# Rotary embedding in a two-branch attention block: how the rotated channels change places

## What is computed

```
def partial_rope(t, pos):
    half = ROT_DIM // 2
    inv_freq = jnp.power(jnp.float32(ROPE_THETA),
                         -jnp.arange(0, ROT_DIM, 2, dtype=jnp.float32) / ROT_DIM)
    ang = pos.astype(jnp.float32)[:, None] * inv_freq[None, :]
    cos = jnp.cos(ang)[None, :, None, :]
    sin = jnp.sin(ang)[None, :, None, :]
    tf = t.astype(jnp.float32)
    x1, x2, rest = tf[..., :half], tf[..., half:ROT_DIM], tf[..., ROT_DIM:]
    out = jnp.concatenate([x1 * cos - x2 * sin, x2 * cos + x1 * sin, rest], axis=-1)
    return out.astype(t.dtype)
...
        h = rms_norm(x, norm_g[layer])
        proj = jnp.einsum('bsd,de->bse', h, w_in[layer])
        (qa, ka, va, za, qb, kb, vb, zb, ga, gb) = jnp.split(proj, split_pts, axis=-1)
        qa = partial_rope(qa.reshape(b, s, A_Q_HEADS, HEAD_DIM), pos)
        ka = partial_rope(ka.reshape(b, s, A_KV_HEADS, HEAD_DIM), pos)
        va = va.reshape(b, s, A_KV_HEADS, HEAD_DIM)
        ya = swa_sink_attention(qa, ka, va, a_sinks[layer]) * jax.nn.silu(za)
```

## Time and profile before

| what | value |
|---|---|
| median of 3 runs | 3460.74 us (3460.51 to 3461.7) |
| the profiled execution, its time | 3458.64 us |
| its span, first to last instruction | 3456.8 us |
| mean granted TensorE clock | 0.999 |
| busy: PE, PEld, DVE, ACT, POOL | 97%, 72%, 43%, 41%, 38% |
| matmuls | 16456 |
| DMA traffic | 319.63 MB, mean 92 GB/s |

### The profile page before, as it was taken

How to read it: one execution, slowest core, us unless ns; L and a number is a source line. 1 busy time by engine, 2 the same in 40 slices (tenths; PEclk the granted TensorE clock), 3 DMA queues, 4 the chain that set the end, 5 groups by cost and what they waited for, 6 DMA issues and landing times.

```text
span 3456.8 us, 48457 instructions
## 1 busy us (share of the span) xinstructions
PE 3369.6 (97%) x16456; PEld 2502.4 (72%) x16456; DVE 1483.7 (43%) x3113; ACT 1432.5 (41%) x2985; POOL 1313.8 (38%) x1087
## 2 busy tenths in 40 slices
PE   7999999999999999999999999999999999999998
PEld 5667866678666786667866678666786667866686
DVE  5561355513554135541355413554135541355412
ACT  4443344433444334443344434444344443444432
POOL 3334432344323443234532344323443234532244
PEclk9999999999999999999999999999999999999999
DMA  4122421224212242122421124212242112421123
GB/s 145 59 68 87 169 92 50 67 87 165 92 50 67 86 166 92 50 67 86 170 87 54 63 86 171 88 54 62 89 168 92 50 62 92 167 90 49 56 91 116
DMA packets 97788, 319.63 MB, mean 92 GB/s; under 512 B 9984, under 2 KB 26624, under 8 KB 95360
## 3 DMA queue, kind: packets, MB, share of 16 engines
q1 hardware_dynamic: 97536, 316.34, 28.1%
HBM read 299.52 MB, written 16.78 MB: 91 GB/s over the span
## 4 chain that ended last, share of the span: by engine, by line
PE 49%; issue 28%; POOL 13%; DVE 7%; ACT 2%; POOLq 0%; DMA 0%; DVEq 0%; ACTq 0%; SPq 0%
POOL w_lo L746 12%; PE acc L876 10%; PE acc L878 8%; PE acc L877 8%; PE ps_o L969 5%; PE ps_pt L937 4%; PE sc L917 2%; PE sc L908 2%; PE sc L876 1%; PE sc L878 1%; PE sc L877 1%; DVE sc L1212 1%; DVE negm L1220 1%; PE acc L978 1%; DVE probs_t L1286 1%
## 5 line engine op out<-in xcount | busy, mean ns | idle before, releaser
L746 POOL TENSOR_TENSOR w_lo<-w_raw,w_hi 128x512 fp32r<-128x512 f32 x928 | 1211.7, 1311 | 2096.0 <-ACT w_hi L1023 2095.9
L876 PE MATMUL acc<-h_hi,w_hi 128*128 128x512 f32 x2688 | 1117.0, 416 | 16.7 <-DVE q L1273 12.4
L878 PE MATMUL acc<-h_hi,w_lo 128*128 128x512 f32 x2688 | 1054.3, 392 | 0.0
L877 PE MATMUL acc<-h_lo,w_hi 128*128 128x512 f32 x2688 | 1050.8, 391 | 0.0
L1023 ACT ACTIVATE w_hi<-w_raw 128x512 fp32r<-128x512 f32 x928 | 573.5, 624 | 333.8 <-DMA w_raw<-w 104.5
L876 PEld LDWEIGHTS acc<-h_hi,w_hi 128*128 128x128 f32 x2688 | 505.0, 188 | 233.7 <-issue 144.0
L878 PEld LDWEIGHTS acc<-h_hi,w_lo 128*128 128x128 f32 x2688 | 504.9, 188 | 112.6
L877 PEld LDWEIGHTS acc<-h_lo,w_hi 128*128 128x128 f32 x2688 | 506.9, 189 | 83.7
L1105 ACT ACTIVATE probs_b<-sc,negm 128x640 f32<-128x640 f32 x256 | 203.6, 795 | 381.3 <-DVE negm L1220 379.6
L1245 DVE SCALAR_TENSOR_TENSOR part<-th,sc 128x512 f32<-128x512 f32 x64 | 43.9, 686 | 566.5 <-PE sc L878 566.5
L1112 ACT ACTIVATE probs_t<-ps_pt 128x512 f32<-128x512 f32 (+1 forms) x272 | 150.6, 554 | 235.2 <-PE ps_pt L937 235.2
(11 more groups left out here) (119 smaller groups left out, 3566.0 us busy)
## 6 DMA issues: line engine op xcount, KB each, us to landing
w_raw<-w SPq DMA_DIRECT2D x464, 512.0 KB, 3.5
rows<-x SPq DMA_DIRECT2D x36, 512.0 KB, 7.7
xt<-x_t SPq DMA_DIRECT2D x16, 1024.0 KB, 9.9
out<-rows SPq DMA_DIRECT2D x32, 512.0 KB, 2.7
x_in<-x SPq DMA_DIRECT2D x28, 512.0 KB, 5.7
cs<-rope_tab SPq DMA_DIRECT2D x8, 512.0 KB, 4.3
bias<-near SPq DMA_DIRECT2D x1, 1024.0 KB, 13.3
g_out<-final_g SPq DMA_DIRECT2D x1, 512.0 KB, 11.3
```

The source lines that it names most:

```text
L746: pool.tensor_tensor(w_lo[n % 2][:, c], w_raw[n % 2][:, c], w_hi[n % 2][:, c].bitcast(FP32), ALU.subtract).then_inc(w_split, 1)
L876: pe.matmul(dst[:, :], hi, src_hi[:, k, :], start=begin, stop=False)
L877: pe.matmul(dst[:, :], hi, src_lo[:, k, :], start=False, stop=False)
L878: mm = pe.matmul(dst[:, :], lo, src_hi[:, k, :], start=False, stop=end)
```

## The change

The matrix, its two products, the rounding to `pre_hi` and the subtraction `pre_lo` are taken out. A new tile `rot` (128 x 512, zero from the start, in place of the two matrix tiles) receives the rotated channels of `pre` by four DMAs of 8 partitions within SBUF, which swap channels 0 to 7 with 8 to 15 of both heads. SP issues them once ScalarE has evicted the tile; they stand in SP's order where the tile's job stands in the plan. The cosine product is written straight to the destination, the sine product is made in place in `rot` with a table whose sign differs for the two halves, and the sum is taken in the destination. The numbers of lines in the file after are its own.

```
+            def swap(b, step):
+
+
+                wait_freed(sp, b, step)
+                for h0 in (0, HD):
+                    for to, src in ((h0, h0 + HALF_ROT), (h0 + HALF_ROT, h0)):
+                        sp.dma_start(rot[to:to + HALF_ROT, :], pre[src:src + HALF_ROT, :]).then_inc(rope_swapped, 16)
...
+            sp.wait_ge(zeroed, 6)
...
+                    elif step[0] == "job" and step[1] in ("k", "q") and step[2] < PAIRS:
+                        swap(b, step)
...
+            pool.memset(rot[:, :], 0.0).then_inc(zeroed, 1)
...
-                    elif kind in ("rope", "rope_k"):
-                        claim(b, step)
-                        pe.wait_ge(rope_lo, b * NROPE + (ROPE_NO[step] + 1))
-                        pe.matmul(bank(step)[:, :], perm_r[:, :], pre_hi[:, :], start=True, stop=False)
-                        pe.matmul(bank(step)[:, :], perm_r[:, :], pre_lo[:, :], start=False,
-                                  stop=True).then_inc(acc_full, 1)
...
-                    wait_freed(act, b, step)
-                    act.activation(pre_hi[:, :], pre[:, :], ACT.Copy).then_inc(rope_hi, 1)
...
                     elif kind in ("rope_in", "rope_in_k"):
-                        no = ROPE_NO[(kind.replace("_in", ""), step[1])]
-                        dve.wait_ge(rope_hi, b * NROPE + (no + 1))
-                        dve.tensor_tensor(pre_lo[:, :], pre[:, :], pre_hi[:, :].bitcast(FP32),
-                                          ALU.subtract).then_inc(rope_lo, 1)
+                        of_k = kind == "rope_in_k"
+                        wait_freed(dve, b, ("job", "k" if of_k else "q", step[1]))
                         dve.wait_ge(cs_in, 16 * (b + 1))
-                        dve.wait_ge(rope_lo, b * NROPE + (no + 1))
-                        dve.tensor_tensor(pre[:, :], pre[:, :], cs[:, 0, :], ALU.mult).then_inc(rope_cos, 1)
+                        if of_k and not first:
+                            wait_kept(dve, b, "keep_k", PAIRS - 1)
+                        dve.tensor_tensor(roped(step), pre[:, :], cs[:, 0, :], ALU.mult).then_inc(rope_cos, 1)
                     elif kind in ("rope", "rope_k"):
-                        s = step[1]
                         no = ROPE_NO[step]
-                        wait_full(dve, b, step)
-                        if kind == "rope_k" and not first:
-                            wait_kept(dve, b, "keep_k", PAIRS - 1)
-                        dst = k_a[:, P:P + BLK] if kind == "rope_k" else q[POS[s] % 2][:, :]
-                        dve.tensor_tensor(dst, bank(step)[:, :], cs[:, 1, :], ALU.mult).then_inc(free(step), 1)
-                        wait_freed(dve, b, step)
+                        dve.wait_ge(rope_swapped, b * (64 * NROPE) + 64 * (no + 1))
+                        dve.tensor_tensor(rot[:, :], rot[:, :], cs[:, 1, :], ALU.mult).then_inc(rope_sin, 1)
                         dve.wait_ge(rope_cos, b * NROPE + (no + 1))
-                        dve.tensor_tensor(dst, pre[:, :], dst, ALU.add).then_inc(rope_done, 1)
+                        dve.wait_ge(rope_sin, b * NROPE + (no + 1))
+                        dve.tensor_tensor(roped(step), roped(step), rot[:, :], ALU.add).then_inc(rope_done, 1)
```

More of the change, by code:

```diff
@@ L31 @@
 HD = 64
+HALF_ROT = HD // 8
 PAIRS = 4
@@ L266, in check_plan @@
     assert [step[1] for step in PLAN if step[:1] == ("mm",) and step[2] == 0] == list(range(NW))
-USES_ACC = ("job", "turn_v", "rope_k", "rope", "norm")
+USES_ACC = ("job", "turn_v", "norm")
 check_plan()
@@ L357, with program @@
 check_ring()
-def program(nc, x, x_t, w, near, far, sinks, norm_g, final_g, gate_b, rope_tab, perm, eye, out):
+def program(nc, x, x_t, w, near, far, sinks, norm_g, final_g, gate_b, rope_tab, eye, out):
     off = [(nc.sbuf_base + 63) // 64 * 64]
@@ L406, in program @@
     pre = at("pre", [P, BLK], FP32, y_lo_at + 4 * BLK * 3)
-    pre_lo = at("pre_lo", [P, BLK], FP32R, y_lo_at + 4 * BLK * 6)
-    pre_hi = at("pre_hi", [P, BLK], FP32R, y_lo_at + 4 * BLK * 7)
     bias = sb("bias", [P, 9, A_KEYS])
@@ L422, in program @@
     ident = sb("ident", [P, P])
-    perm_raw = sb("perm_raw", [P, P])
-    perm_r = sb("perm_r", [P, P], FP32R)
+    rot = sb("rot", [P, BLK])
     far_sb = sb("far_sb", [P, 8])
@@ L480, in program @@
     pair_valued = sem("pair_valued")
-    rope_hi = sem("rope_hi")
-    rope_lo = sem("rope_lo")
+    rope_swapped = sem("rope_swapped")
     rope_cos = sem("rope_cos")
+    rope_sin = sem("rope_sin")
     rope_done = sem("rope_done")
@@ L512, in program @@
     c_dve = sem("c_dve")
-    N_CONSTS = 6
+    N_CONSTS = 5
     ADDED = HALVES * TT - O_BANKED
@@ L676, in _ @@
             load_w(0, 1)
-            for dst, src in ((perm_raw[:, :], perm), (g_out[:, :], final_g), (bias[:, 0:8, :], near), (far_sb[:, :], far),
+            for dst, src in ((g_out[:, :], final_g), (bias[:, 0:8, :], near), (far_sb[:, :], far),
                              (sink_sb[:, :], sinks), (gb_raw[:, :], gate_b)):
@@ L722, in _ @@
             pool.memset(v_b[:, 0:TT, :], 0.0).then_inc(zeroed, 1)
-            pool.wait_ge(zeroed, 5)
+            pool.memset(rot[:, :], 0.0).then_inc(zeroed, 1)
+            pool.wait_ge(zeroed, 6)
             def rsqrt(which, t, n, got, got_count, mid, done, count):
@@ L817, in _ @@
             turn_rstd(0)
-            pe.wait_ge(zeroed, 5)
+            pe.wait_ge(zeroed, 6)
             def token_products(b, n, c):
@@ L1178, in _ @@
             dve.wait_ge(consts_in, 16 * N_CONSTS)
-            dve.tensor_copy(perm_r[:, :], perm_raw[:, :]).then_inc(c_dve, 1)
             dve.tensor_scalar(gb_half[:, :], gb_raw[:, :], 0.5, None, ALU.mult).then_inc(c_dve, 1)
@@ L1184, in _, with roped @@
             dve.memset(bias[:, 8, :], 0.0).then_inc(c_dve, 1)
-            dve.wait_ge(c_dve, 11)
+            dve.wait_ge(c_dve, 10)
             dve.memset(bias[0:CHUNK, :, A_KEYS - CHUNK:A_KEYS], NEG).then_inc(c_dve, 1)
             dve.memset(bias[CHUNK:P, 8, CHUNK:P], NEG).then_inc(c_dve, 1)
-            dve.wait_ge(c_dve, 13)
+            dve.wait_ge(c_dve, 12)
+            def roped(step):
+                return k_a[:, P:P + BLK] if step[0].endswith("_k") else q[POS[step[1]] % 2][:, :]
             def shape_scores(b, first, s, t, hh):
@@ L1361, in rope_tables @@
     tab[0] = 1.0
-    perm = np.zeros((P, P), np.float32)
     for h0 in (0, HD):
         for i in range(half):
-            for c in (h0 + i, h0 + half + i):
+            for c, sign in ((h0 + i, -1.0), (h0 + half + i, 1.0)):
                 tab[0, c] = np.cos(ang[:, i])
-                tab[1, c] = np.sin(ang[:, i])
-            perm[h0 + half + i, h0 + i] = -1.0
-            perm[h0 + i, h0 + half + i] = 1.0
+                tab[1, c] = sign * np.sin(ang[:, i])
     tab = tab.reshape(2, P, NBLK, BLK).transpose(2, 1, 0, 3)
-    return np.ascontiguousarray(tab), perm
+    return np.ascontiguousarray(tab)
 def kernel(x, norm_g, w_in, a_sinks, b_rel_bias, w_br_a, w_br_b, gate_bias, w_out, final_g):
@@ L1411 @@
     far = np.ascontiguousarray(np.broadcast_to(b_rel_bias[0][:, 2 * P], (P, 8)))
-    rope_tab, perm = rope_tables()
+    rope_tab = rope_tables()
     arrays = {
@@ L1419 @@
         "gate_b": np.ascontiguousarray(gate_bias[0].reshape(2 * KT, P).T),
-        "rope_tab": rope_tab, "perm": perm, "eye": np.eye(P, dtype=np.float32),
+        "rope_tab": rope_tab, "eye": np.eye(P, dtype=np.float32),
     }
```

## The result

| what | before | after |
|---|---|---|
| median of the runs, us | 3461.07 (4 runs, 3460.51 to 3461.7) | 3486.41 (4 runs, 3483.12 to 3488.37) |
| the profiled execution, its time, its span, us | 3458.64, 3456.8 | 3488.37, 3486.6 |
| mean granted TensorE clock | 0.999 | 0.989 |

The ratio of after to before is 1.0074, with a 95% interval of 1.0061 to 1.0087: the change costs 25 us where I had forecast a gain of 26, and the time lies 30 us above the upper end of my range.

A forecast was written before the change was run, and what follows sets the result against it. TensorE was taken to bound the kernel; 22 us from q1 to q3, 0 from the lead and 4 from block 0 gave 26 off 3458.64, so 3432.6, stated as 3435 with 2.1 for the median; range 3400 to 3456.

The forecast's parts named there:

- q1 to q3: 24 rotations inside the attention steps: each gains 0.93 us as ScalarE's tanh and copy come earlier, 22 us in all.
- The pitch: SP's queue: issues some 0.53 us apart, so four take 2.1 and the weight load is asked for at 932.45.
- The landing: Weight load behind the four DMAs: needs 3.3 to 4.1 us, median 3.5, so it lands at 935.95.
- The following one waits for `w_lo` in any case: SP's queue in q1 to q3: only one load is held up; the next waits for GpSimd's `w_lo` anyway.
- slower: Rival, chance 0.09: SP issues at 1.34 us pitch delay weight loads; 24 rotations lose 2.3 us each, about 3525 us.
- three signs: Would make it wrong: `rot` wait over a microsecond, issue pitch over 0.76, or q0's scores starting over 2 us off.
- lead: q0 and k0, blocks 1 to 7: VectorE's chain sets the scores' start; gain 0, 1.5 us either way, 7 times.
- block 0: First block's lead: TensorE's 2.91 us wait for `pre_lo` and the products go, with 0.46 for q0: 4 us gained.
- one long wait in place of two short ones: Lead, blocks 1 to 7: TensorE waits once, behind the sum of q0, 2 to 4 us a block.
- The turn came 0.6 us earlier: q1 to q3: the copy of turned weights ends at 933.13 instead of 933.73, so TensorE is 0.6 us earlier.
- Landing of the small DMAs: Swapping DMAs into `rot`: taken as 3.3 us from weight loads, landing at 935.3; nothing late under 3.8 us.
- VectorE's waits for `rot` near none: Sign expected in the profile after: VectorE hardly waits for the swapped channels.

The follow-up runs named there:

- experiment 2: Kernel before, permutation kept, plus four idle copies of 8 partitions within SBUF where the change has its swaps, behind the same wait: 3479.62 us, ratio 1.0057.
- Experiment 4: Changed kernel plus six unread products ahead of the turn that waits behind z1, z2 and z3, 33 us more work: 3468.72 us, ratio 1.003 to before.
- experiment 1: Changed kernel with each group of four swapping DMAs issued after the next weight load, not ahead of it: 3431.13 us, ratio 0.9919 to before.
- experiment 5: Changed kernel, swap behind the next weight load, and the last row product of the block before moved later in the plan: 3412.52 us, ratio 0.9856 to before.
- experiment 6: Changed kernel, swap behind the next weight load, and k0's sine product and sum moved to the second quarter of q0: 3431.28 us, ratio 0.9917 to before.
- experiment 7: Changed kernel, swap behind the next weight load, with both the last row product and k0's sine product and sum moved later: 3413.02 us, ratio 0.9862 to before.
- experiment 8: Kernel before, permutation kept, with only the last row product of the block before moved later in the plan: 3455.84 us, ratio 0.9985.

## Why the prediction was wrong

The step that failed is the term of **q1 to q3**: "the load is asked for at 932.45", and behind it that it lands 3.5 us later, at 935.95, and that TensorE then waits "some 0.7". Measured from `pre`'s start, that is an issue at 2.75 and a landing at 6.25; after showed an issue at 3.31 to 3.44, a landing at 6.9 to 7.2 in 17 rotations and at 8.1 to 9.0 in 7, and TensorE waiting 1.0 to 1.4 us in 14 of the 17, 3.0 in block 0's three, and 2.2 to 3.1 in the 7. Three things were wrong or missing, in the order of the chain.

1. *The pitch.* I took 0.53 us for an issue, from weight loads. An issue of `rot` takes 0.62 us and the next starts 0.67 to 0.72 after it, in all 24 rotations. The row of SP's queue, after:

```profile
L670 SPq DMA_DIRECT2D rot<-pre x160: 624/625/797, 27.2 to 3231.4; - x160
```

That made each load 0.66 us later than I said, and the tanh 0.7 later (7.52 from `pre`'s start, where I had 6.8). This term alone ate most of the 0.93 us that I counted for each: in blocks 1 to 7 the rotation of q1, which met no packet of 16 KB, gained 0.16 us each (q1 to q2, 416.6 us in place of 417.7).

2. *The landing.* I took "3.3 to 4.1, median 3.5" from the earlier trace rows. That line is of the 20 loads between 900 and 1100 us only; the same line for all 464 of before is

```profile
DMA to landing us min/median/max: 3.3/3.5/10.8
```

and the loads that met a packet, 4.07 to 4.64 us in q2 of before, were there to be seen. *"The following one waits for `w_lo` in any case"* held for its own time: it started 3.9 us after `pre`'s start in blocks 1 to 6, before 4.0. What it left out is that the first load, asked for 8 us ahead of it before, now goes some 0.5 us ahead (3.41 and 3.90 in q2), so two loads share the DMA engines in every rotation. In 17 of 24 that did not matter (3.44 to 3.93 us, where I had 3.5). In the other 7 an instruction packet was there too, and the load took 4.7 to 5.6, more than with a packet alone. I had no term for a load that takes longer, and six of the seven make most of the loss of q2. Why a packet meets these loads in after and none in experiment 2 is open.

3. *The clock.* The prediction has no sentence on it. Behind waits of TensorE of 2.5 to 3.1 us it went to half, 15 times. Experiment 4 shows 18 us of that by itself. Of the 15, seven stand in leads, five behind a load that met a packet and three, in block 0, behind one that did not. How the 25 us divide between the queue and the packets no run shows; that the waiting swaps ahead of the load are needed for the loss, experiment 1 does.

The rival *slower* had the right mechanism, "SP's queue", and I gave it 0.09, because I set its turning point at 0.76 us for an issue. The pitch stayed under it, at 0.68. The turning point was worked out with a fixed landing time and a full clock; with either of the last two points it lies lower, and the loss came in below it. Of the three signs that I had named as making the forecast wrong, only a wait for `rot` of over a microsecond is there, and that one does no harm (below).

Of the **lead**: block 0 from k0 to q0 gave 3.6 us (forecast 4). In blocks 1 to 7, 0.5 us less from k0 to q0 and 1.4 more from q0 to the scores, so 0.9 a block worse, inside the 1.5 either way around the 0 that I took. The sine product was stretched as the two-input products of the earlier trace rows were, to 1.77 us; but "one long wait in place of two short ones" behind the sum of q0 was wrong. TensorE waits for the eviction of v0 (19.0 us), since with z0's load late the squares and row products came later still, and VectorE evicts v0 behind one of them. Behind each of these seven waits, too, the clock went to half. In experiment 1, where z0's load isn't late, the forecast's long wait for the sum of q0 is there: 16.2 us, 7 times.

**What held.** The permutation's waits went. The turn came 0.6 us earlier. The cosine product beside `w_lo` took 1.40 us and ended 0.55 behind it, as the row of the lead had it. *Landing of the small DMAs*: where VectorE waited for `rot`, the sine product started 1.99 us after the fourth issue's start, 8 times in after, and 1.95 to 2.07 in experiment 1, against the bound of 3.3 from the weight loads. "VectorE's waits for `rot` near none" holds for q1 to q3, not for k0, whose swap it waits for in blocks 1 to 7, 2.4 to 3.3 us each, nor for q0 of block 0 (1.6). These waits do no harm: experiments 1 and 5 have them too (22.0 and 22.8 us). The row of after:

```profile
DVE rot L1274 <- DMA rot<-pre: 22.4, 8, 3.3
```

A gain of 22 us in the rotations was also there to be had, as experiment 1 showed; it needed the load ahead of the swap. That it is the forecast's 24 x 0.93 to the microsecond is luck: it came as 21 x 1.07, with TensorE and not the load setting the tanh, and nothing in block 0.

## What to carry to other kernels

On an in-order queue, a DMA that waits for a result of compute should stand behind the prefetches, not ahead of them; moving each group of four such copies behind one load was worth 55 us of 3486. When a change makes the main engine earlier, judge the lateness of everything else against the new time at which it is wanted: the same four issues ahead of the load cost nothing in q1 to q3 of the kernel before, in a run in which no load met an instruction packet, and 27 us against before in the changed one, packets and clock included, which with the load ahead of them gains 22 there. And a wait of 2 to 3 us on TensorE is to be priced with the clock that may fall behind it, some 1.5 us more each time by experiment 1. Last, a median of 20 loads is no bound: the slow ones were in the same trace.

## What the runs showed of the hardware

- Issuing a copy of 8 partitions within SBUF kept SP's queue for 0.625 us, at a pitch of 0.67 to 0.72 in the rotations, whether it held 4 KB (experiment 2) or 16; a load of 128 partitions and 512 KB took 0.33. I had expected the small one to be no dearer.
- Such a copy was in use 1.95 to 2.07 us after its issue started (after and experiment 1).
- One 16 KB packet of instruction fetch went with 4.7 to 5.6 us for a 512 KB load in place of 3.44 to 3.93, where a second load stood 0.49 us behind (after, 7 times of 7), and with 4.07 to 4.64 in place of 3.38 to 3.65 for a load alone (before, 8 times of 8). No experiment set the packet, so this is what went together and not a shown cause.
- In after the granted clock went to half behind 15 of 16 waits of 2.5 to 3.1 us in leads and in q1 to q3. The length of the wait does not decide it: in block 0 the same three waits of 2.9 us had no fall behind them in experiments 1 and 6, two in experiment 5 and three in experiment 7; 2.3 to 2.4 us in experiment 1's leads had one in four of seven, 1.9 us in experiment 8's in four of seven.
- A stretch of 3.4 us at half clock behind such a wait cost 1.5 us (42.0 against 40.5 in experiment 1) and 1.6 (12.7 against 11.1 from q0 to the scores in experiment 8).
- A VectorE product or sum of 128 x 512 with both inputs in SBUF took 0.69 us by itself, and 1.57 to 1.82 where GpSimd's `w_lo` ran beside it (experiment 1).
